# Expert slabs in halves of the contraction, and row stores on ScalarE's queue, in a two-layer trunk with a mixture of experts

## The reference

```python
gate = one_hot(g_idx) * (g_w * within)          # top-1 group, top-2 experts in it
a = jnp.einsum("nd,edf->nef", t, lw["moe_w1"])  # d = 1024, f = 512
b = jnp.einsum("nd,edf->nef", t, lw["moe_w3"])
y = jnp.einsum("nef,efd->nd", jax.nn.silu(a) * b * gate[..., None], lw["moe_w2"])
x = x + g2 * y
```

## Time and profile before

| | us |
|---|---|
| median of 3 runs | 1246.88 |
| lowest, highest | 1239.22, 1247.97 |
| profiled execution, its own time | 1246.88 |
| its span | 1245.0 |
| TensorE busy in matmuls | 1110.2 (89%) |
| VectorE, ScalarE, GpSimd busy | 561.3, 290.4, 94.7 |
| moved by DMA | 333.27 MB |

### The profile page before, as it was taken

The page is one execution under the profiler, slowest core; times in us unless marked ns, Lnnn a source line. Parts: engine busy times, 40 slices in busy tenths (PEclk is TensorE's granted clock), DMA queues, the critical chain, the costliest instruction groups (busy, mean ns, idle before and its releaser), DMA issues.

```text
span 1245.0 us, 18459 instructions
## 1 busy us (share of the span) xinstructions
PE 1110.2 (89%) x7505; PEld 546.5 (44%) x7505; DVE 561.3 (45%) x1436; ACT 290.4 (23%) x717; POOL 94.7 (8%) x112
## 2 busy tenths in 40 slices
PE   4899998698998999888789999968999899997776
PEld 1465544375456333222235655435755733332222
DVE  1266886466347311211162678945744732111124
ACT  0247412223122110000021772132331311100000
POOL 0020002210001000000021000040000100000001
PEclk9899999899999999988989999978999899998988
DMA  8570134877936999999973103374495499999995
GB/s 356 194 192 1 68 93 125 263 279 272 397 146 237 427 412 416 426 428 427 419 269 112 66 27 102 117 175 186 169 386 206 162 420 426 400 428 427 428 426 195
DMA packets 76967, 333.27 MB, mean 268 GB/s; under 512 B 28095, under 2 KB 30535, under 8 KB 58439
## 3 DMA queue, kind: packets, MB, share of 16 engines
q1 hardware_dynamic: 69479, 308.04, 63.0%
q0 software_dynamic: 7392, 23.93, 5.8%
HBM read 314.38 MB, written 17.56 MB: 267 GB/s over the span
## 4 chain that ended last, share of the span: by engine, by line
PE 73%; DMA 15%; DVE 5%; issue 3%; ACT 3%; SPq 1%; another core or an unknown queue 0%; DVEq 0%; ACTq 0%
PE bank L565 69%; DMA ring<-in_moe_w_dram 10%; PE bank L568 4%; DMA ring<-in_w_in_dram 2%; ACT arena L1465 2%; DMA ring<-in_ada_w_dram 1%; DVE x L1786 1%; DMA ring<-in_w_out_dram 1%; DVE arena L1778 1%; DVE ring L1786 1%; DVE x L1778 1%; DVE small L1786 0%; DVE small L2100 0%; DVE hT L1778 0%
## 5 line engine op out<-in xcount | busy, mean ns | idle before, releaser
L565 PE MATMUL bank<-ring,arena 128*32 128x512 f32 (+1 forms) x2240 | 381.1, 601 | 26.4 <-issue 12.1
L565 PE MATMUL bank<-arena 128*32 128x512 f32 (+3 forms) x1632 | 305.5, 564 | 27.3 <-issue 15.5
L1465 ACT ACTIVATE arena<-bank 128x512 f32<-128x512 f32 (+3 forms) x302 | 128.8, 473 | 596.3 <-PE bank L568 411.2
L565 PE MATMUL bank<-ring,hT 128*128 128x512 f32 x576 | 257.8, 603 | 5.7 <-DMA ring<-in_w_in_dram 2.8
L565 PEld LDWEIGHTS bank<-ring,arena 128*32 128x32 f32 (+1 forms) x2240 | 113.1, 116 | 216.3 <-issue 216.1
L565 PEld LDWEIGHTS bank<-ring,hT 128*128 128x128 f32 x576 | 109.4, 194 | 134.2 <-issue 128.9
L565 PEld LDWEIGHTS bank<-arena 128*32 128x32 f32 (+2 forms) x1632 | 90.0, 123 | 107.1 <-issue 92.4
L1778 DVE TENSOR_TENSOR arena<-bank,mrow 128x512 f32<-128x512 f32 x36 | 24.9, 692 | 233.6 <-PE bank L565 220.9
L565 PE MATMUL bank<-hT,ring 128*128 128x384 f32 x384 | 128.2, 488 | 0.0
L565 PEld LDWEIGHTS bank<-hT,ring 128*128 128x128 f32 x384 | 71.2, 190 | 46.8 <-issue 1.3
L568 PE MATMUL bank<-const,arena 128*128 128x128 f32 x443 | 66.6, 286 | 20.8 <-DVE arena L1778 10.1
(11 more groups left out here) (157 smaller groups left out, 852.4 us busy)
## 6 DMA issues: line engine op xcount, KB each, us to landing
ring<-in_moe_w_dram SPq DMA_DIRECT2D x60, 2048.0 KB, 19.5
arena<-in_moe_w_dram SPq DMA_DIRECT2D x36, 2048.0 KB, 22.6
ring<-in_ada_w_dram SPq DMA_DIRECT2D x24, 2048.0 KB, 8.9
ring<-in_w_in_dram SPq DMA_DIRECT2D x14, 2048.0 KB, 9.7
ring<-in_w_out_dram SPq DMA_DIRECT2D x4, 2048.0 KB, 10.4
expert_dram<-arena SPq DMA_DIRECT2D x16, 512.0 KB, 19.6
tok_dram<-arena POOLq DMA_DIRECT2D x6, 512.0 KB, 2.9
arena<-in_na_rpb_dram SPq DMA_DIRECT2D x16, 96.0 KB, 7.0
```

Of the source, the lines that this page charges most:

```text
L565: return nc.tensor.matmul(out, lhsT, rhs, start=start, stop=stop)
L1465: return nc.scalar.activation(out, in_, func, **kw)
```

## The change

Each slab becomes two pieces of 1 MB, the first and the second half of the contraction (rows k of the matrix), so 128 rows of 8 KB each. The eight slots become sixteen half slots with a semaphore each. TensorE waits for a piece before each half of a phase and signals after each half; SyncE frees and loads half slots. For y, the first half of the contraction runs over both column halves, then the second half. `MOE_SLOTS` names the slots in another order. Row stores are issued by ScalarE on its own queue (`rows_out`). `direct` does the first column half of all three tiles before the second. The rest adapts counts and frees semaphores.

```diff
-MOE_SLOTS = [1, 2, 5, 4, 0, 6, 3, 7]
+MOE_SLOTS = [2, 5, 4, 1, 0, 6, 3, 7]
...
-        for p in sorted(set(holders(n))):
-            slab = (p, "aby".index(what))
-            if slab not in needed:
-                needed.append(slab)
-            if last[p] == n:
-                given_back.append((slab, (what, n)))
+        for half in range(2):
+            for p in sorted(set(holders(n))):
+                piece = (p, "aby".index(what), half)
+                if piece not in needed:
+                    needed.append(piece)
+                if last[p] == n:
+                    given_back.append((piece, (what, n, half)))
...
+        def piece_at(i):
+            return slot(MOE_SLOTS[i // 2])[:, i % 2 * SLAB // 2:(i % 2 + 1) * SLAB // 2]
...
-        moe_in = [sem(f"moe_in{i}") for i in range(len(MOE_SLOTS))]
+        moe_in = [sem(f"moe_in{i}_{half}") for i in range(len(MOE_SLOTS)) for half in range(2)]
...
                     def results(n):
-                        w = batch_slabs(l, n - first, 2)
                         if n == first:
                             pe.wait_ge(es["list_taken"], 4 * l + 4)
                         pe.wait_ge(es["hT"], n + 1)
+                        w = batch_pieces(l, n - first, 2, 0)
                         for half in range(2):
                             if n:
                                 pe.wait_ge(es["y"], n * 2 + half - 1)
-                            down(half, holders(n - first), w).then_inc(es["y_full"], 1)
+                            last = down(half, holders(n - first), w, (0, 1))
+                        last.then_inc(es["y_full"], 1)
+                        w = batch_pieces(l, n - first, 2, 1)
+                        for half in range(2):
+                            down(half, holders(n - first), w, (2, 3)).then_inc(es["y_full"], 1)
...
                     def second_product(n):
-                        w = batch_slabs(l, n - first, 1)
-                        up(bank[3], (n - first) % 2, holders(n - first), w).then_inc(es["b_full"], 1)
+                        for half in range(2):
+                            w = batch_pieces(l, n - first, 1, half)
+                            up(bank[3], (n - first) % 2, holders(n - first), half, w).then_inc(es["b_full"], 1)
...
-                        for half in range(2):
-                            pe.wait_ge(es["y"], 2 * (l + 1) * BATCHES - 1 + half)
+                    for half in range(2):
+                        pe.wait_ge(es["y"], 2 * (l + 1) * BATCHES - 1 + half)
+                        for t in range(TILES):
                             mm(direct_banks[l, t][half][:], late_w[:, t, :],
                                y_e[:, 1, half * 512:(half + 1) * 512]).then_inc(done, 1)
...
                 for phase in PHASES:
                     what, n_ = phase
-                    freed = [slab for slab, phase in LOADS[len(MOE_SLOTS):] if phase == (what, n_)]
-                    n_ += l * BATCHES
                     ahead = [j for at, j in AHEAD if at == phase and l + 1 < DEPTH]
-                    if freed or ahead:
-                        sp.wait_ge(es[{"a": "a_full", "b": "b_full", "y": "y_full"}[what]], 2 * n_ + 2 if what == "y" else n_ + 1)
-                    for slab in freed:
-                        load(slab)
-                    if what == "y" and n_ < (l + 1) * BATCHES - 1:
-                        store_y(es, n_, y_buffer(n_ - l * BATCHES), n_ - l * BATCHES)
+                    for half in range(2):
+                        freed = [piece for piece, at in LOADS[2 * len(MOE_SLOTS):] if at == (what, n_, half)]
+                        m_ = n_ + l * BATCHES + 1
+                        if freed or (half and ahead):
+                            if what != "y":
+                                sp.wait_ge(es[{"a": "a_full", "b": "b_full"}[what]], 2 * m_ - 1 + half)
+                            else:
+                                sp.wait_ge(es["y_full"], 3 * m_ - 2 * (1 - half))
+                        for piece in freed:
+                            load(piece)
...
+                def rows_out(n_):
+
+                    c_ = n_ - l * BATCHES
+                    act.wait_ge(es["y"], n_ * 2 + 2)
+                    act.dma_start(expert_dram[c_ * P:(c_ + 1) * P, :],
+                                  y_e[:, y_buffer(c_), :]).then_inc(es["y_stored"][y_buffer(c_)], 16)
...
                     if n_ + 1 < end:
                         tokens_T(es, n_ + 1, (n_ + 1 - first) % 2, n_ < 1)
+                    if n_ > first:
+                        rows_out(n_ - 1)
```

138 lines of the change are left out of this document (75 added, 63 removed).

## The result

The changed kernel takes 1236.76 us, the kernel before on the same chips 1244.58 us (medians of 20 runs each): ratio 0.9934, 95% interval [0.9915, 0.9953]. That is 7.8 us less, where I had forecast 2.0 us more. The profiled execution took 1233.34 us (span 1231.4 us).

What follows compares the result with a forecast made beforehand. Transfers were taken to bound both expert stages, plus TensorE's work behind the last slab. The kernel's 1246.9 us plus 0.8 us in layer 1 and 1.2 in layer 0 gave 1248.9 us, range 1235 to 1257.

Steps and rivals of the forecast that it cites:

- What bounds the kernel: Both expert stages: each ends when its late transfers are through, plus TensorE's work behind the last slab.
- Halves and the stream: Each stage's stream: 8 KB packets take 0.8% more time per byte, +1.8 us a layer; earlier release gives -0.5 us.
- The starved spot: Layer 0's stream, 460 to 470, DMA share 0.95: the emptiest window; earlier release was taken to gain 0.5 us.
- The tail gain: Batch 8's last two products: with halves less work follows the last piece, -5.3 us in layer 1, -4.9 in layer 0.
- the slow restart: TensorE after some 4 us idle: matmuls run slowly at first, costing 1.4 us in y8's second half.
- The gathers ahead of the last pieces: End of each stage: early row store lets gathers overtake; last piece lands at 1225.6, TensorE waits some 4 us.
- the row by which I had two queues share one for one: Window 622.5 to 630, 452 packets against 510: read as equal sharing, so the remaining slab stream takes 1.5 times as long.
- The wait on "remote": Before VectorE's last read of y8 in layer 0: 5.26 us, unexplained, nothing counted from it.
- A: Stage ends: gathers start too late or take too little, so the tail's gain comes through; 1236.7 us, chance 0.27.
- B: Batches 5 to 8: many waits lower TensorE's clock, +16 us, 1265 us; chance 0.06.
- C: Stage streams: each transfer pays a fixed part, +68 us a layer, 1383 us; chance 0.01.
- D: Expert stages: pieces arrive pairwise together and waits end as before, only costs remain; 1252 us, chance 0.08.

Runs made afterwards that it cites:

- the repeat: The changed kernel, unchanged, timed and profiled a second time: 1236.48 us, ratio 0.9924 to the kernel before.
- hoist_pe: The changed kernel with TensorE's last four phases of a layer moved ahead of its branch on the fullest expert: 1235.42 us, ratio 0.9920.
- stores_act: The kernel before, whole slabs kept, with only the row stores moved to ScalarE's queue: 1247.93 us, ratio 1.0012.

## Why the prediction was wrong

**What bounds the kernel.** The stages are bound by their transfers, right; that the bound reaches into b8 and y8 was wrong. Of the two ends of b8's wait I read only the transfer. The earlier trace rows hold 2.12 us of "issue" between the landing and b8, and the earlier trace rows 4.06 us of idling: the branch. In the kernel before it ends together with the transfer in layer 0 and 2.1 us behind it in layer 1, and with pieces it follows y7 as before.

**Halves and the stream** (+1.8 - 0.5 us a layer). Both terms were too small, and they nearly cancel. Pieces are 1.4% slower to carry (428 against 422 GB/s), my figure was 0.8%; over 228 us that is 3.2 us. The starved spot gave back 10 GB/s over 50 us, which is 1.2. The difference is 2.0 for my 1.3. The Trainium skill's figure of 341 GB/s for a 1 MB transfer (DMA: Bandwidth & Descriptors, Bandwidth) does not hold for 1 MB pieces queued behind one another: 422 GB/s here.

**The tail gain** (b8 ends at 1214.4 in layer 1). This step failed: b8 ended at 1217.0 on that clock, because it cannot start before the branch is through (1208.2), and then pays the slow restart (8.80 us for 7.1), which my sum has as well. In layer 0 b8 ended at 619.0, where it had ended before (618.9). The finer waits work one phase earlier: without the one in y7 the stages are 11.7 us longer and the whole gain is gone. In layer 0 what they bring there only makes good for what the pieces and the overtaking stores cost.

**The gathers ahead of the last pieces** (+4.7 us for the last piece, then a wait of 4 us and a restart of 1.4). This step decided the sign, and it failed on its sizes. The store was issued 1.2 us later than I had it (1205.2, not 1204), it landed in 9.1 us, not 5.4, and the first gather moved data some 3.3 us after its issue, not 2: so the gathers began at about 1217.6, not 1211.5, and could hold up only the rest of the stream. The last piece landed at 1222.3 in the repeat, 3.3 us ahead of my 1225.6, and TensorE ended y8's first half at 1221.7 and 1223.2 in two profiles, 0.3 and 1.8 us later than my 1221.4. What is left of the wait of 4 us and the restart of 1.4 is 0 to 0.65 us. The mechanism is real: with the branch out of the way the wait is 2.43 and 2.13 us, the second with its restart. Of the row by which I had two queues share one for one I misread the window: in its first 1.5 us the slabs run alone (270 packets of one queue, none of the other), and in its last 2.5 the gathers, so 452 against 510 says nothing. The rule itself holds in the changed kernel's 626 to 632, where both queues have work all through:

```profile
q0 software_dynamic: 419, 1.52, 64.9%
q1 hardware_dynamic: 429, 0.88, 38.2%
```

It does not hold while the last pieces run out: in 1208 to 1211 it is 210 packets of the gathers against 61. With the measured beginning my sum gives (1220.9 - 1217.6) x 1.5 = 5.0 us and a landing at 1222.6, with the stream's 2.0 us in place of 1.3 one at 1223.6; measured are 1222.3 and, in `hoist_pe`, 1222.1.

**A term that I put at nothing.** The wait on "remote" ahead of 631.51 I could not explain and did not count. It came in one of three profiles of the kernel before, cost 2.8 us there, and was in the 631.51 from which I reckoned layer 0. What it is stays open.

**The sum.** +1.2 and +0.8 us were forecast for layers 0 and 1; over three profiles each the stages are 1.1 and 4.3 us shorter. These 5.4 us are the larger part of the 7.8 timed; the rest of the span is 3.3 us shorter in the same profiles, which its spread of 10 us does not tell from chance. That my figure was near zero came of two large terms with opposite signs, the tail gain and the gathers, which were both too large.

**The rivals.** A gave 1236.7 and the kernel takes 1236.76; that is luck. A started from 1246.9, and the kernel before takes 1244.58 over 20 runs, so A forecast a gain of 10.2 us where 7.8 came; and it had 5.3 us in layer 1 and 4.9 in layer 0, from b8 and y8, where the stages gained 4.3 and 1.1. B, more waits and a lower clock, did not come: the granted clock in 550 to 600 is 1.00, 0.96 and 0.93 in three profiles, for 0.88, 0.93 and 0.90 before. C and D did not occur: transfers queue without a pause, and from 516 to 606 TensorE has 8 or 9 waits of 1.4 us on average that end at a transfer, where the kernel before has 2 or 3 of 1.5 to 2.2.

## What to carry to other kernels

When a stage streams its operands at the limit of the DMA engines, what counts is how much work is left behind the landing that TensorE last waits for, so look for the last phase that does wait, not for the last phase; a branch, like any fixed pause behind it, hides a later landing that is shorter than the pause. Splitting the wait helps there by half a phase and by the slow restart that a long wait brings, splitting the release of buffers in a full stream brought nothing measurable here. Take the reference from more than one profile: one late read of 2.8 us in the first profile of the kernel before looked like half of the gain. Before you price an overtaking transfer, fix the time at which it begins to move data and the moment at which its victim is needed: here 6 us in the one and up to 2 us in the other decided the sign.

## What the runs showed of the hardware

- TensorE behind its waits: 64 matmuls took 8.72 us behind 5.87 us of idling (granted clock 0.73 in that 10 us) and 8.80 behind 4.17 us. The length of one wait does not tell it alone: in the changed kernel the 32 matmuls behind a wait of 2.12 us (581.61) took 3.64, in the kernel before the 64 behind one of 2.12 us (578.25) took 8.8; and in `hoist_pe` the 32 of y8's second half took 3.64 behind 2.43 us and 5.34 behind 2.13 us. In the stretch 550 to 600 of the first profiles TensorE was busy 37.8 us at a granted clock of 1.00 with short waits, and 42.9 us at 0.88 with long ones: less busy time, higher clock. The repeats lie closer together (39.8 us at 0.96 and 41.6 at 0.93 with short waits, 39.0 at 0.93 and 43.2 at 0.90 with long ones).
- Matmuls inside the branch begin 3.8 to 5.2 us behind the last one ahead of it; in `hoist_pe`, with them ahead of the branch, they begin 1.3 us behind it, when their operand has landed.
- A 0.5 MB store on its own queue lands in 8.3 us (median) beside a full stream of 8 KB packets and in 11.0 us beside one of 16 KB packets (`stores_act`); behind the 8 KB stream on the same queue it takes 21.6 us.
- Where two queues had work throughout (626 to 632 of the changed kernel) they shared the engines packet by packet: 419 packets of the gathers (4 KB) against 429 of the slabs (2 KB), 64.9% and 38.2% of the engines' time.
- Outside the expert stages, the same kernel's profiles differ by up to 10 us (793.6 to 803.2 for the kernel before), within them by 1.5, and by 2.7 for the changed kernel.
